# Value products of a sparse-attention decode step: full-array prompt products, and 64 stationary columns by 512 for the samples

## The reference

```python
def sparse_attend(q, k_sel, v_sel, q_pos, k_pos, rel_bias):
    logits = jnp.einsum('bthd,btkhd->bhtk', q, k_sel).astype(jnp.float32) * ATTN_SCALE
    ...
    p = jax.nn.softmax(logits, axis=-1).astype(v_sel.dtype)
    out = jnp.einsum('bhtk,btkhd->bthd', p, v_sel)
```

## Time and profile before

| | us |
|---|---|
| median of 3 runs | 1863.84 |
| lowest, highest run | 1859.91, 1866.31 |
| span of the profiled execution | 1871.8 |
| PE busy in the span | 1726.3 (92%) |
| DVE, ACT, POOL busy | 859.4, 653.4, 603.9 |

### The profile page before, as it was taken

How to read it: one execution, slowest core, us unless ns; L and a number is a source line. 1 busy time by engine, 2 the same in 40 slices (tenths; PEclk the granted TensorE clock), 3 DMA queues, 4 the chain that set the end, 5 groups by cost and what they waited for, 6 DMA issues and landing times.

```text
span 1871.8 us, 28982 instructions
## 1 busy us (share of the span) xinstructions
PE 1726.3 (92%) x11176; PEld 1413.1 (75%) x11176; DVE 859.4 (46%) x1839; ACT 653.4 (35%) x1374; POOL 603.9 (32%) x715
## 2 busy tenths in 40 slices
PE   7888999989967778898789999999999999999998
PEld 6553464789944455565555689999999999999997
DVE  4571889757734444566531343323132323232324
ACT  4464786577232233343321121222222222222123
POOL 1100334266354665555513140404040404040400
PEclk9799999989987899998889999999999999999999
DMA  8301202111184655655571001111110101020202
GB/s 242 93 1 49 92 31 78 49 35 42 43 270 149 177 173 160 175 152 152 149 260 66 0 1 46 46 46 45 39 50 29 60 20 70 10 80 3 98 1 96
DMA packets 68965, 158.03 MB, mean 84 GB/s; under 512 B 9402, under 2 KB 25518, under 8 KB 68608
## 3 DMA queue, kind: packets, MB, share of 16 engines
q1 hardware_dynamic: 47488, 84.91, 13.7%
q0 software_dynamic: 21376, 71.75, 12.8%
HBM read 144.14 MB, written 12.49 MB: 84 GB/s over the span
## 4 chain that ended last, share of the span: by engine, by line
PE 82%; DVE 6%; issue 4%; another core or an unknown queue 3%; ACT 3%; POOL 2%; DMA 1%; SPq 0%; DVEq 0%; ACTq 0%; POOLq 0%
PE psum L1819 7%; PE psum L1817 7%; PE psum L1806 7%; PE psum L1807 7%; PE psum L1805 7%; PE psum L1818 7%; PE psum L1746 6%; PE psum L1360 5%; PE psum L1524 4%; PE psum L1373 3%; PE psum L1549 2%; PE psum L1663 2%; PE psum L1340 2%; PE psum L1641 2%
## 5 line engine op out<-in xcount | busy, mean ns | idle before, releaser
L1805 PE MATMUL psum<-n_hi,wup_hi 128*128 128x384 f32 (+1 forms) x768 | 251.3, 327 | 0.0
L1817 PE MATMUL psum<-h_hi,wdn_hi 128*128 128x384 f32 (+1 forms) x768 | 250.9, 327 | 0.0
L1807 PE MATMUL psum<-n_hi,wup_lo 128*128 128x384 f32 (+1 forms) x768 | 250.8, 327 | 0.0
L1806 PE MATMUL psum<-n_lo,wup_hi 128*128 128x384 f32 (+1 forms) x768 | 250.8, 327 | 0.0
L1819 PE MATMUL psum<-h_hi,wdn_lo 128*128 128x384 f32 (+1 forms) x768 | 250.2, 326 | 0.0
L1818 PE MATMUL psum<-h_lo,wdn_hi 128*128 128x384 f32 (+1 forms) x768 | 250.1, 326 | 0.0
L2441 DVE TENSOR_TENSOR h_lo<-h_full,h_hi 128x384 fp32r<-128x384 f32 (+1 forms) x96 | 112.5, 1184 | 261.5 <-ACT h_hi L1221 252.8
L1213 ACT ACTIVATE hrelu<-psum 128x384 f32<-128x384 f32 (+1 forms) x96 | 45.5, 474 | 502.0 <-PE psum L1807 502.0
L2446 DVE TENSOR_TENSOR x_region<-psum,x_region 128x384 f32<-128x384 f32 (+1 forms) x192 | 102.8, 536 | 252.9 <-PE psum L1819 251.8
L905 POOL TENSOR_TENSOR wup_lo<-wup_full,wup_hi 128x4096 fp32r<-128x4096 f32 x8 | 72.3, 9037 | 421.0 <-ACT wup_hi L1197 421.0
L1075 ACT ACTIVATE arena<-x_region,arena 128x384 bf16<-128x384 f32 (+2 forms) x192 | 166.5, 871 | 23.3 <-POOL arena L851 23.3
(11 more groups left out here) (329 smaller groups left out, 3155.1 us busy)
## 6 DMA issues: line engine op xcount, KB each, us to landing
wup_full<-in_w_up SPq DMA_DIRECT2D x8, 2048.0 KB, 8.0
wdn_full<-in_w_down SPq DMA_DIRECT2D x8, 2048.0 KB, 7.7
arena<-in_x_prompt SPq DMA_DIRECT2D x16, 512.0 KB, 8.8
arena<-in_w_in SPq DMA_DIRECT2D x3, 2048.0 KB, 8.4
arena<-in_w_in SPq DMA_DIRECT2D x12, 512.0 KB, 5.6
out<-arena SPq DMA_DIRECT2D x17, 256.0 KB, 4.5
arena<-in_w_out SPq DMA_DIRECT2D x8, 512.0 KB, 8.4
out<-arena SPq DMA_DIRECT2D x8, 512.0 KB, 2.7
```

The costliest lines, as they stand in the source:

```text
L1805: pe.matmul(b, wu_hi[:, k, col], n_hi[:, k, o:o + w], start=(k == 0), stop=False)
L1806: pe.matmul(b, wu_hi[:, k, col], n_lo[:, k, o:o + w], start=False, stop=False)
L1807: i = pe.matmul(b, wu_lo[:, k, col], n_hi[:, k, o:o + w], start=False, stop=(k == KT - 1))
L1817: pe.matmul(b, wd_hi[:, f, col], h_hi[:, hf, 0:w], start=(f == 0), stop=False)
```

## The change

Prompt values: for each block of keys one product with 128 stationary columns (both heads' value columns) by 256 moving ones (both heads' queries). It computes both heads' queries against both heads' values, so half of its result isn't wanted; `take_values` copies the two wanted 64 x 128 blocks with two instructions. Sample values: for each page one product with 64 stationary columns (the rows of both groups of heads) by 512 moving ones (all eight heads), two per tile, both into partitions 0 to 63 of bank 7. `near_vals` has two products in place of six. DVE scales and masks with two instructions of 32 partitions, and `fold` reads 64 partitions in place of 128. The counts of `pv_done` are halved.

```diff
@@ sp
-            sp.wait_ge(pv_done, 2 * NPR)
+            sp.wait_ge(pv_done, NPR)
@@ act even_turn (odd_turn on DVE alike)
-                act.wait_ge(pv_done, 2 * q)
+                act.wait_ge(pv_done, q)
@@ pe fold
-                    i = pe.matmul(bank(6)[:, 448 + 8 * k:456 + 8 * k], od[:, c * P:(c + 1) * P],
-                                  const[:, K_SQ + hh * DS:K_SQ + (hh + 1) * DS], start=True, stop=True)
+                    i = pe.matmul(bank(6)[:, 448 + 8 * k:456 + 8 * k], od[0:64, c * P:(c + 1) * P],
+                                  const[0:64, K_SQ + hh * DS:K_SQ + (hh + 1) * DS], start=True, stop=True)
@@ pe near_vals
-                for g in range(4):
-                    pe.matmul(bank(7)[32 * g:32 * g + 32, 0:256], PTw[0:SMP, 32 * g:32 * g + 32],
-                              V[0:SMP, NT - 1, 256 * (g % 2):256 * (g % 2) + 256], start=True, stop=False, skip_group_check=True)
+                pe.matmul(bank(7)[0:64, :], PTw[0:SMP, 0:64], V[0:SMP, NT - 1, :], start=True, stop=False, skip_group_check=True)
                 pe.wait_ge(near_in[1], 16 * b + 16)
-                for hh in range(2):
-                    i = pe.matmul(bank(7)[32 * hh:32 * hh + 32, 0:256], PTn[:, 32 * hh:32 * hh + 32], vring[:, r % 4, 0, 256 * hh:256 * hh + 256],
-                                  start=False, stop=False, skip_group_check=True)
-                i.then_inc(v_used, 1)
+                pe.matmul(bank(7)[0:64, :], PTn[:, 0:64], vring[:, r % 4, 0, :], start=False, stop=False,
+                          skip_group_check=True).then_inc(v_used, 1)
@@ pe vals
-                for g in range(4):
-                    kk, hh = divmod(g, 2)
-                    i = pe.matmul(bank(7)[32 * g:32 * g + 32, 0:256], PTd[:, n % 2, x % 2 * P + 32 * g:x % 2 * P + 32 * g + 32],
-                                  ring[:, r % 4, kk, 256 * hh:256 * hh + 256],
-                                  start=False, stop=(x == NPAGE_TILES - 1), skip_group_check=True)
+                for kk in range(2):
+                    c = x % 2 * P + 64 * kk
+                    i = pe.matmul(bank(7)[0:64, :], PTd[:, n % 2, c:c + 64], ring[:, r % 4, kk, :],
+                                  start=False, stop=(x == NPAGE_TILES - 1 and kk == 1), skip_group_check=True)
                 i.then_inc(v_used, 1)
@@ pe values
                 for k in range(i_ + 1):
-                    for e in range(2):
-                        i = pe.matmul(bank(3)[64 * e:64 * e + 64, 0:P], V[:, k, (2 * hp + e) * HD:(2 * hp + e + 1) * HD],
-                                      probT[:, e, k, :], start=(k == 0), stop=(k == i_), skip_group_check=True)
-                        if k == i_:
-                            i.then_inc(pv_done, 1)
+                    i = pe.matmul(bank(3)[:, 0:2 * P], V[:, k, 2 * hp * HD:(2 * hp + 2) * HD], probT[:, :, k, :],
+                                  start=(k == 0), stop=(k == i_), skip_group_check=True)
+                i.then_inc(pv_done, 1)
@@ dve take_values
-                dve.wait_ge(pv_done, 2 * q + 2)
-                dve.tensor_copy(mixT[:, hp, i_ * P:(i_ + 1) * P], bank(3)[:, 0:P]).then_inc(val_taken, 1)
+                dve.wait_ge(pv_done, q + 1)
+                for e in range(2):
+                    own = slice(64 * e, 64 * e + 64)
+                    i = dve.tensor_copy(mixT[own, hp, i_ * P:(i_ + 1) * P], bank(3)[own, e * P:(e + 1) * P])
+                i.then_inc(val_taken, 1)
@@ dve, after a sequence's last values
-                    dve.scalar_tensor_tensor(out=od, in0=bank(7)[:, 0:256], scalar=drs[:, b % 2:b % 2 + 1],
-                                             in1=own_head, op0=ALU.mult, op1=ALU.mult).then_inc(od_ready, 1)
+                    for hh in range(2):
+                        own = slice(32 * hh, 32 * hh + 32)
+                        i = dve.scalar_tensor_tensor(out=od[own, :], in0=bank(7)[own, 256 * hh:256 * hh + 256], scalar=drs[own, b % 2:b % 2 + 1],
+                                                     in1=own_head[own, :], op0=ALU.mult, op1=ALU.mult)
+                    i.then_inc(od_ready, 1)
```

More of the change, by code:

```diff
@@ L2312, in odd_turn @@
                 dve.wait_ge(pt_ready, PIECES_TO[q] + 2 * e + 2)
-                dve.wait_ge(pv_done, 2 * q)
+                dve.wait_ge(pv_done, q)
                 dve.tensor_copy(probT[:, e, 4:i_ + 1, :], bank(2).rearrange("p (a b) -> p a b", a=4)[:, 0:i_ - 3, :]).then_inc(pt_dve, 1)
```

## The result

The changed kernel takes 1915.8 us (median of 4 runs, 1911.0 to 1918.0) where the kernel before takes 1865.1 in runs beside it: ratio 1.027 [1.0244, 1.0295], +50.7 us. The forecast was 1937 us, +73. The profiled execution has a span of 1914.3 us, 42.5 more than before's.

A forecast was written before the change was run, and what follows sets the result against it. The prediction took PE, with holes in the attention stage, as nearest to the bound: 120 us of added work, 107 after the clock, less 34 for holes, gave +73 on 1863.8, so 1937 us, range 1890 to 1978.

The forecast's parts named there:

- A tile: Sample values in the attention stage: two 64x512 products one after the other, 1.83 us in place of 0.54, +82.6 us.
- a block of keys: Prompt values in the attention stage: one 128x256 product takes 0.43 us in place of 0.215, +31 us over 144 blocks.
- The sum: PE work added in the attention stage at full clock: prompt values 28, sample values 82.6, near values 6, DVE 3; 120 us.
- The overlap rival: Sample values: a tile's two 64x512 products run side by side in 0.97 us; +7 us, 1871 us, chance 0.05.
- The fixed 0.175 us: Prompt values: fixed time of each of 32 runs may go, 0 to -5.6 us; -3 taken.
- the holes: PE's idle in the attention stage takes part of the added work: 34 us, bounds 0 and 77.
- the clock: Attention stage: lower clock makes work dearer, fuller PE has fewer drops; middle taken, 120 x 1.06 - 20 = 107 us.
- the long stops: Attention stage: PE, ACT and DVE all stand for up to 6.5 us, cause unnamed; nothing counted on to come back.
- Softmax waits (L1663): PE's waits in the attention stage that have value products in between; they will shrink, no separate size given.
- the wait at L1582: PE waits before a turn for DVE's copy of prompt values; doesn't shrink, grows by 8 times 0.29 us.
- The later release of POOL's gathers: Longer sample-value products release POOL's gathers later; priced at 0, since gathers are issued several steps ahead of use.
- the rival in which all is paid: Attention stage: idle isn't where the added work is and the clock stays as it is; +136 us, 2000 us, chance 0.11.

The follow-up runs named there:

- prompt_only: The changed kernel with the sample-value parts of the kernel before, so only the prompt-value half of the change; +17.6 us over the kernel before (1.0097).
- sample_only: The kernel before with only the sample-value half of the change, prompt values as before; +66.8 us over the kernel before (1.0378).
- sample_halves: sample_only with the second page's 64x512 product sent to partitions 64 to 127, so on different columns; +25.4 us over the kernel before (1.0146).
- The fillers: The kernel before with one or three extra, unread 128x256 products in front of each tile's four sample products; +24.4 and +73.9 us over the kernel before.
- after_split: The changed kernel with each 64x512 sample product cut into two of 64x256; +98.8 us over the kernel before (1.0551).
- after_again: The changed kernel, unchanged, profiled beside the kernel before on one chip of the second kind; +97.0 us over the kernel before (1.0547).

## Why the prediction came out as it did

**The added work was sized nearly right.** A tile was to take 1.83 us and takes 1.86; a block of keys 0.43 and takes 0.43. The sum said 120 us of PE's time; the traces give 112 on one chip and 118 on the other, and most of that difference is in the work of the kernel before (318 and 310 us for the same products). By part, prompt_only adds 22 where the sum had 28, and sample_only 95 where it had 89. The sum had no term for the key logits in front of a tile's values, which grew by 0.10 us each, 6 us in all. The overlap rival is out in the changed kernel, and sample_halves shows under which condition it would hold.

On the figure of 131 ns for 512 columns (the Trainium skill, TensorE: Matmul & The Clock Gate, Part 2): with four passes per float32 product (the Trainium skill, FP8 and Floating Point Precision, TensorE Precision Notes) the tile's 1.86 us are 8 passes of 0.23 us, so the measurement is near that page's other value, 216 ns for an isolated matmul, and 131 doesn't hold here.

**The fixed 0.175 us went altogether.** Five blocks take 2.16 us, which leaves 0.01 beside 5 x 0.43. I had taken half. The fillers paid 0.20 us before the next line and 0.13 around them. The Trainium skill, TensorEngine Tiling, Tiling Modes (Key Properties), says that a change of tiling mode drains the engine. The traces agree with that in the direction of all these figures; no run shows that a drain is their cause.

**The step that was mis-sized is what comes back.** The forecast took 34 us for the holes; idle fell by 45. It took the middle for the clock, 120 x 1.06 - 20 = 107, so 13 us; the clock gave 29 (44 us lost to it before, 15 after). Both were too small for the chip of the forecast's runs, which makes 38 of the profile where I had 73. The reason for holding back was the long stops, of which I said that I count on nothing. They did shrink: the chain's "another core or an unknown queue" in the stage went from 12.0% of 440 us to 3.8% of 482, 53 to 18 us. The lower clock goes with them: in the changed kernel the three longest stops ended at 590.9, 643.5 and 699.4 us, and the lower level was granted from 592.5, 643.7 and 701.7 us on. The traces overstate the return a little. The measured medians differ by 50.7 us and the two profiled executions by 42.5, because before's profiled execution was some 8 us over the median of its runs and the changed kernel's was not. By the medians 112 - 51 = 61 us came back, not 74, against the 47 of the forecast.

**What holes take was right in kind.** Softmax waits (L1663) fell from 19 to 4 us, the wait at L1582, which was not to shrink, is still there with 9.4 us (13.5 before), and the key logits' waits are as before (26 and 28 us). The key turns' waits went from 20 us to nothing. They were the second largest of PE's waits, and I had not spoken of them. The later release of POOL's gathers cost nothing, as priced: PE doesn't wait for gathered rows in the changed kernel.

**What I could not see** was that the price isn't the change's own: +51 us on one chip and +97 on another, for the same 112 to 118 us of work. The forecast's +73 lies between the two. That 1915.8 us falls inside its range of 1890 to 1978 is owed to the width of the range, which holds an error of 21 us, and not to the two terms for what comes back. On the second chip the holes gave 16 us and the clock 2, half and a seventh of what I took, and the result lies between the forecast and the rival in which all is paid. That rival kept the lower clock of these rows in its price (x 1.13), which that chip doesn't have.

**Open.** What the long stops are. On the first kind of chip PE, ACT and DVE stand together while POOL goes on for most of the time (in the one that ends at 585.4 us it issues three more gathers and then stands for 2.1 us too), and the wide products had fewer of them. Whether a fuller PE, fewer instructions or chance did that isn't shown: the runs made for it fell on chips without stops.

## What to carry to other kernels

Count array time as columns streamed, and ask which products stand on different columns or rows of the array at once: four 32-column products side by side take 0.54 us, little more than the 0.43 of one. Replacing products side by side by fewer, wider ones halved the count here. It doubled the time of a block of prompt values (0.215 to 0.43 us) and more than tripled that of a tile's sample values (0.54 to 1.86 us). Look at the line in front of a changed product too. Before pricing PE work against idle, ask what makes the idle, and whether another chip has it: the idle of one profiled execution need not be a property of the kernel.

## What the runs showed of the hardware

- The same program differed by about 5% between chips (1777 and 1865 to 1875 us), all of it in the stage with gathers: 355 against 455 us, with 7 against 106 us at the lower clock.
- A full-array float32 product put between products on 32-column groups costs 0.33 us beside its columns: 0.20 in its own line, 0.10 in the line before it and 0.03 in the line behind.
- Two 64x512 float32 products take 1.01 us on different columns and 1.86 us on the same ones.
- DVE copies of 64 partitions by 128 take 288 ns each, those of 128 partitions 286: halves cost as much as the whole.
- A 64x512 product cut into two of 64x256 costs the same, weight loads included: a tile takes 1.82 us up to the next line in after_split and 1.81 in after_again.
